# Sample scores woven into the prompt's attention, and output products between the sample's values

## The reference, cut to what matters

```
z = rmsnorm(x) @ w_in            # u | q | k | v, 4 heads, q and k in two halves of 64
s = q @ k / 8 - slope * dist     # per head and half; masked where dist < 0
p = softmax(s)
o = (p[half 0] - lam * p[half 1]) @ v
o = rmsnorm(o) * g * 0.8
x = x + [pool_out ; o] @ w_out
x = x + moe_top4of32(rmsnorm(x)) # router, 32 experts, clamped SwiGLU
y = rmsnorm(x)
```

## Time and profile before

| | us |
|---|---|
| median of 3 runs | 1681.72 |
| lowest, highest | 1679.38, 1684.91 |
| the profiled execution's own time | 1682.89 |
| its span | 1681.1 |
| TensorE busy | 1542.0 (92%) |
| VectorE busy | 1223.2 (73%) |
| ScalarE busy | 1004.1 (60%) |

### The profile page before, as it was taken

One profiled execution on the slowest core, in us unless ns is written; L12 is line 12 of the kernel. 1 busy time (PEld: TensorE's weight loads), 2 busy tenths in 40 slices (PEclk: granted clock), 3 DMA queues, 4 the chain that ended last, 5 costly groups with the idle time before them and its releaser, 6 DMA issues.

```text
span 1681.1 us, 23490 instructions
## 1 busy us (share of the span) xinstructions
PE 1542.0 (92%) x7948; PEld 1275.0 (76%) x7949; DVE 1223.2 (73%) x1035; ACT 1004.1 (60%) x894; POOL 435.1 (26%) x404
## 2 busy tenths in 40 slices
PE   5799669997599999999999999999999999999960
PEld 5799344887478888888888888888888888888850
DVE  3312860226478888888888888888888888888848
ACT  4322554014367677767767776776776677677632
POOL 1000000000422332333233233223323322332311
PEclk9899679998799999999999999999999999999985
DMA  7233115431588999999999999999999999998936
GB/s 219 84 101 115 64 51 160 160 129 60 233 307 340 360 355 345 360 359 364 361 361 356 346 360 357 366 359 363 358 346 363 358 365 357 361 360 343 354 108 257
DMA packets 93472, 475.98 MB, mean 283 GB/s; under 512 B 14410, under 2 KB 27354, under 8 KB 43665
## 3 DMA queue, kind: packets, MB, share of 16 engines
q1 hardware_dynamic: 81689, 449.85, 71.4%
q0 software_dynamic: 11744, 25.61, 4.0%
HBM read 468.62 MB, written 23.74 MB: 293 GB/s over the span
## 4 chain that ended last, share of the span: by engine, by line
PE 84%; DVE 8%; DMA 3%; ACT 2%; issue 1%; POOL 1%; SPq 0%; POOLq 0%; DVEq 0%; ACTq 0%
PE ps L1614 62%; PE ps L1350 8%; PE ps L1593 3%; PE ps L1619 3%; PE ps L1511 2%; DVE arena L1314 2%; PE ps L1487 2%; DVE lo L940 1%; DMA raw<-w_in 1%; PE ps L1472 1%; PE ps L1587 1%; ACT hi L642 1%; DMA arena<-h_rows,idx_g 1%; DVE arena L1037 1%; DVE stats L1041 1%
## 5 line engine op out<-in xcount | busy, mean ns | idle before, releaser
L940 DVE TENSOR_TENSOR lo<-raw,hi 128x2048 fp32r<-128x2048 f32 x268 | 605.7, 2289 | 129.9 <-ACT hi L642 129.8
L642 ACT ACTIVATE hi<-raw 128x2048 fp32r<-128x2048 f32 x268 | 499.0, 1909 | 107.3 <-PE ps L1614 65.1
L1614 PE MATMUL ps<-hi,t_hi 128*128 128x512 f32 x1536 | 447.6, 400 | 6.9 <-DVE t_lo L1217 5.2
L1614 PE MATMUL ps<-lo,t_hi 128*128 128x512 f32 x1536 | 434.8, 391 | 0.0
L1614 PE MATMUL ps<-hi,t_lo 128*128 128x512 f32 x1536 | 434.4, 391 | 0.0
L1614 PEld LDWEIGHTS ps<-lo,t_hi 128*128 128x128 f32 x1536 | 289.7, 189 | 62.9
L1614 PEld LDWEIGHTS ps<-hi,t_lo 128*128 128x128 f32 x1536 | 289.9, 189 | 61.4
L1614 PEld LDWEIGHTS ps<-hi,t_hi 128*128 128x128 f32 x1536 | 280.4, 189 | 70.5 <-DVE lo L940 11.4
L940 DVE TENSOR_TENSOR lo<-arena,hi 128x2048 fp32r<-128x2048 f32 x128 | 290.3, 2288 | 20.8 <-ACT hi L642 20.7
L642 ACT ACTIVATE hi<-arena 128x2048 fp32r<-128x2048 f32 x128 | 245.4, 1917 | 47.1 <-PE ps L1614 46.1
L577 POOL COPY idx_g<-idx 128x1 uint32 (+1 forms) x34 | 71.7, 2110 | 361.2 <-PE ps L1593 328.3
(11 more groups left out here) (223 smaller groups left out, 1391.0 us busy)
## 6 DMA issues: line engine op xcount, KB each, us to landing
raw<-w SPq DMA_DIRECT2D x256, 1024.0 KB, 5.7
arena<-w SPq DMA_DIRECT2D x128, 1024.0 KB, 7.5
raw<-w_in SPq DMA_DIRECT2D x8, 1024.0 KB, 5.5
raw<-cache_k SPq DMA_DIRECT2D x32, 256.0 KB, 3.5
raw<-cache_v SPq DMA_DIRECT2D x32, 256.0 KB, 3.3
raw<-w_out SPq DMA_DIRECT2D x4, 1024.0 KB, 4.9
arena<-expert_rows SPq DMA_DIRECT2D x2, 2048.0 KB, 14.1
hi<-expert_rows SPq DMA_DIRECT2D x2, 2048.0 KB, 22.9
```

Of the source, the lines that this page charges most:

```text
L642: act_e.activation(hi[:, slot, :], raw_at(slot_raw), ACT.Copy).then_inc(s_hi, 1)
L940: v.tensor_tensor(lo[:, slot, :], raw_at(slot_raw), hi[:, slot, :].bitcast(F32), ALU.subtract).then_inc(s_lo, 1)
L1614: last = pe.matmul(ps[:, base_bank + b, :], lhs[l][:, row, :], r[:, ck.slot(j), at:at + 512], start=first_k and kk == 0 and q == 0, stop=F ...
```

## The change

The sample's 32 page steps no longer follow the attention: two are placed ahead of its loop and two in each step. For this the PSUM banks are dealt anew: the scores have two banks (one step) instead of four, the transposed weights one instead of two, the values bank 3, the transposed page one instead of three. ScalarE's copies of the pages (`page_t`) stand one ahead and one behind `weights_t` in each step. The products with the new keys are a block of their own behind the loop (`new_key_scores`). For a finished column block, `o_squares`, `o_norm` and `o_lo` move from steps 1, 2 and 4 behind it to steps 0, 1 and 3. The table of the sample's weights (`p_t`) is laid out with a wider step. Behind the loop both sample softmaxes precede `o_norm(3)`, `out_product(0)` starts the next stage, sequences 4 to 7 of the values are placed between the router's work, and the last `choose` steps are in another order. POOL's reloads of x wait for the new-key scores in addition.

```diff
+        B_AT, B_PV, B_KT = 2, 3, 4
+
+        def o_bank(i):
+            return 5 if i < 4 else 7
...
             pool.wait_ge(s_qb, 2)
             pool.wait_ge(s_sss, NB * H)
+            pool.wait_ge(s_nk, 1)
             reload_x(2, s_xr[1])
...
+            def page_t(m):
+                act_e.wait_ge(s_kp, m + 1)
+                if m >= 2:
+                    act_e.wait_ge(s_sss, m - 1)
+                act_e.activation(kt_s[:, m % 2, :], ps[:, B_KT, :], ACT.Copy).then_inc(s_kc, 1)
+
+            page_t(0)
+            page_t(1)
+            for i in range(16):
+                exponents(i)
+                if i < 15:
+                    page_t(2 * i + 2)
+                weights_t(i)
+                if i < 15:
+                    page_t(2 * i + 3)
+                if i >= 5 and i % 4 == 1:
+                    o_root(i // 4 - 1, P)
+                if i >= 7 and i % 4 == 3:
+                    o_hi(i // 4 - 1)
...
+            sample_exp(0)
             sample_exp(1)
+            o_root(3, P)
+            o_hi(3)
...
             bias_max(0)
+            sample_queries()
             for i in range(16):
                 if i + 1 < 16:
                     bias_max(i + 1)
                 weights(i)
-                if i == 2:
-                    sample_queries()
+                if i % 4 == 0 and i >= 4:
+                    v.wait_ge(s_pv, i)
+                    o_squares(i // 4 - 1)
                 if i % 4 == 1 and i >= 5:
-                    v.wait_ge(s_pv, i - 1)
-                    o_squares(i // 4 - 1)
-                if i % 4 == 2 and i >= 6:
                     o_norm(i // 4 - 1)
-                if i % 4 == 0 and i >= 8:
-                    o_lo(i // 4 - 2)
-            o_lo(2)
+                if i % 4 == 3 and i >= 7:
+                    o_lo(i // 4 - 1)
...
             sample_softmax(0)
             sample_softmax(1)
+            o_norm(3)
+            residual(0)
+            o_lo(3)
             sample_weights(0)
-            residual(0)
-            v.wait_ge(s_kp, NB * H + 4 * H)
-            o_squares(4)
-            o_norm(4)
-            sample_weights(1)
-            residual(1)
             start = Chunks(PRO, 0)
             v.wait_ge(s_late2, 64)
             v.memset(before[:, 0, :], 0.0)
             link(v.memset(sel, 0.0))
             norm2(0)
-            o_lo(4)
+            residual(1)
+            sample_weights(1)
+            norm2(1)
+            v.wait_ge(s_kp, NB * H + 4 * H)
+            o_squares(4)
             residual(2)
-            norm2(1)
+            o_norm(4)
+            norm2(2)
+            choose(0)
+            choose(1)
             v.wait_ge(s_kp, 2 * NB * H)
             o_squares(5)
             o_norm(5)
+            o_lo(4)
             residual(3)
             o_lo(5)
-            norm2(2)
-            choose(0)
-            residual(4, (0, 1))
             norm2(3)
-            choose(1)
-            residual(4, (2, 3))
+            choose(2)
+            residual(4)
             norm2(4)
-            choose(2)
             choose(3)
             choose(4)
...
-                if i >= 2:
-                    pe.wait_ge(s_sb, i - 1)
+                if i >= 1:
+                    pe.wait_ge(s_sb, i)
...
-                if m >= 3:
-                    pe.wait_ge(s_kc, m - 2)
+                if m >= 1:
+                    pe.wait_ge(s_kc, m)
...
+            def new_key_scores():
+                pe.wait_ge(s_ate, 16)
+                for m in range(NB * H):
+                    b, h = m // H, m % H
+                    rows = slice(32 * (b % 4), 32 * (b % 4) + 32)
+                    last = pe.matmul(ps[rows, B_AT, 32 * (b // 4):32 * (b // 4) + 32], q_blk[:, m, :], k_t[:, h, 512:544], start=h == 0, stop=h == H - 1,
+                                     tile_position=(0, 32 * (b % 4)))
+                last.then_inc(s_nk, 1)
+
+            pe.wait_ge(s_pl, 4)
+            scores(0)
+            page_transposes(0)
+            scores(1)
+            sample_scores(0)
+            sample_scores(1)
...
+            for i in range(16):
+                if i + 2 < 16:
+                    scores(i + 2)
+                if i >= 1:
+                    values(i - 1)
+                if i < 15:
+                    sample_scores(2 * i + 2)
+                weight_transposes(i)
+                if i < 15:
+                    sample_scores(2 * i + 3)
+            values(15)
+            new_key_scores()
...
+            out_product(0)
+            o_transposes(3, P)
+            sample_transposes(0)
+            out_product(1)
+            sample_transposes(1)
+            for b in range(4):
+                sample_values(b)
             out_product(2)
             pe.wait_ge(s_late2, 64)
             h2_transposes(0)
-            out_product(3)
+            sample_values(4)
             router(0)
+            sample_values(5)
+            h2_transposes(1)
+            sample_values(6)
+            router(1)
+            sample_values(7)
+            o_transposes(4, P)
+            out_product(3, (0, 1))
+            h2_transposes(2)
+            out_product(3, (2, 3))
             o_transposes(5, P)
-            h2_transposes(1)
+            router(2)
             out_product(4, (0, 1))
-            router(1)
-            h2_transposes(2)
-            out_product(4, (2, 3))
-            router(2)
             h2_transposes(3)
+            out_product(4, (2,))
+            router(3)
+            out_product(4, (3,))
             h2_transposes(4)
-            router(3)
             router(4)
```

More of the change, by code:

```diff
@@ L734, in o_hi, with exponents @@
                     act_e.activation(sample_cols(t_hi, i - 4), every_32(src), ACT.Copy).then_inc(s_oh_, 1)
+            def exponents(i):
+                nk = P * (i // 4 + 1)
+                act_e.wait_ge(s_mx, i + 1)
+                for c in range(2):
+                    w = pr[:, 2 * (i % 2) + c, 0:nk]
+                    e = act_e.activation(w, w, ACT.Exp, bias=st[:, 20 + 2 * (i % 2) + c:21 + 2 * (i % 2) + c],
+                                         accum_out=st[:, 24 + 2 * (i % 2) + c:25 + 2 * (i % 2) + c])
+                e.then_inc(s_e, 1)
             def weights_t(i):
@@ L741, in weights_t @@
                     act_e.wait_ge(s_pv, i - 1)
[L742 to L759, removed]
+                act_e.activation(at_sb[:, i % 2, 0:nk], ps[:, B_AT, 0:nk], ACT.Copy).then_inc(s_ate, 1)
+            def page_t(m):
[16 more added lines that the diff above has]
+                    o_hi(i // 4 - 1)
             act_e.wait_ge(s_ust, 32)
@@ L1425, in scores, with weight_transposes @@
                 nk = P * (qt + 1)
-                if i >= 2:
-                    pe.wait_ge(s_sb, i - 1)
+                if i >= 1:
+                    pe.wait_ge(s_sb, i)
                 for c in range(2):
                     rows = slice(HD * c, HD * c + HD)
-                    last = pe.matmul(ps[:, 2 * (i % 2) + c, 0:nk], q_t[rows, h, P * qt:P * qt + P], k_t[rows, h, 0:nk], start=True, stop=True)
+                    last = pe.matmul(ps[:, c, 0:nk], q_t[rows, h, P * qt:P * qt + P], k_t[rows, h, 0:nk], start=True, stop=True)
                 last.then_inc(s_sc, 1)
+            def weight_transposes(i):
+                pe.wait_ge(s_a, i + 1)
+                if i >= 1:
+                    pe.wait_ge(s_ate, i)
+                for k in range(i // 4 + 1):
+                    last = pe.transpose(ps[:, B_AT, P * k:P * k + P], aa[:, i % 2, P * k:P * k + P], ident)
+                last.then_inc(s_atr, 1)
             def o_transposes(i, n):
@@ L1476, in _, with sample_scores @@
[L1476 to L1479 removed]
+            def sample_scores(m):
                 b, h = m // H, m % H
[L1481 to L1482 removed]
                 if m + 1 < NB * H:
                     page_transposes(m + 1)
+                if m == 0:
+                    pe.wait_ge(s_qb, 2)
                 pe.wait_ge(s_kc, m + 1)
                 rows = slice(32 * (b % 4), 32 * (b % 4) + 32)
[L1487 to L1489 removed]
+                pe.matmul(ps[rows, 6 + b // 4, :], q_blk[:, m, :], kt_s[:, m % 2, :], start=h == 0, stop=h == H - 1,
@@ L1548, in router @@
                 last.then_inc(s_lg, 1)
-            for t in range(2):
-                sample_transposes(t)
-                out_product(t, (0, 1))
-                sample_values(4 * t)
-                out_product(t, (2, 3))
-                for b in range(4 * t + 1, 4 * t + 4):
-                    sample_values(b)
-            o_transposes(4, P)
+            out_product(0)
[5 more added lines that the diff above has]
+                sample_values(b)
             out_product(2)
```

108 lines of the change are left out of this document (41 added, 67 removed).

## The result

| | kernel before | changed kernel |
|---|---|---|
| median | 1681.01 us (4 runs, 1679.38 to 1684.91) | 1700.58 us (4 runs, 1699.02 to 1701.97) |
| span of the profiled execution | 1681.1 us | 1697.2 us |
| mean granted clock | 0.955 | 0.961 |

The ratio is 1.012, 95% interval 1.010 to 1.014: **slower by some 20 us**, where 2.2 us less were forecast, and outside the range of 1670 to 1691. The forecast is wrong, and the sign with it.

What follows compares the result with a forecast made beforehand. VectorE was taken to bound the attention, TensorE the page stage and the woven loop. 12.0 us gained in the loop, less 3.8 behind it and 6 for clock falls, left 2.2 us gained: 1679.5 us, range 1670 to 1691.

Steps and rivals of the forecast that it cites:

- loop with its block: Woven attention loop through the new-key scores: 109.0 us at full clock where it was 121.0, 12.0 us gained.
- part two: From behind the new-key scores to the router's running sums: 3.8 us lost at full clock.
- the clock falls (two and one): TensorE clock drops at long stalls: three of five possible places, 2 us lost each, 6 us together.
- After that each wait that I followed had been met: Behind the wait in out_product(0), TensorE's followed waits, norm2 among them, were already met: no further loss.
- Content without the new-key scores: TensorE's own work in the woven loop at full clock, apart from the new-key products: 74.5 us.
- The new-key block: 32 new-key products in a block behind the loop, 0.155 us each: 5.0 us.
- The wait in every step: Second page transposition waits for ScalarE's page copy behind weights_t: 0.9 to 1.25 us in 15 steps, 15.8 us.
- The norm of o: TensorE stalls at steps 5, 9 and 13 while VectorE's o_norm awaits ScalarE's root: 8.5 us together.
- `o_lo` and the ends: Score waits at steps 7 and 11, the last step's weights, and the start: 5.2 us together.
- The wait in `out_product(0)`: Third chunk waits for the first residual, behind both softmaxes and o_norm(3) on VectorE: 3.9 us.
- The tail: From the last output product to the router's running sums: 9.1 us, 5.0 less than before.
- the rival by which it does not come back: TensorE's clock stays at 0.50 early in the woven loop, with later falls: slower, 1692 us; chance 0.20.

Runs made afterwards that it cites:

- store ahead of the wait: Changed kernel with GpSimd's stores of h2 of tiles 0 and 1 issued ahead of the wait for the sample's last value; 1679.61 us, 0.9984 of before.
- store in its place, loads behind it: Changed kernel with SyncE's first expert-weight loads also waiting until the first store of h2 has landed; 1691.05 us, 1.0049 of before.
- part one alone: Changed kernel's woven loop and new-key block, then the earlier kernel's order except two output-product chunks and o_transposes(3) moved ahead; 1679.64 us, 0.9981 of before.
- pages first: "store ahead of the wait" with both page copies of a step ahead of the transposed weights' copy on ScalarE; 1671.32 us, 0.9940 of before.
- norm later: "pages first" with o_norm one step later on VectorE and o's transpositions one step later on TensorE; 1665.25 us, 0.9907 of before.
- residual first: "norm later" with residual(0) split and its first chunks placed earlier in VectorE's queue, behind each softmax; 1660.89 us, 0.9864 of before.
- page before the exponentials: "residual first" with the first page copy ahead of the exponentials on ScalarE at steps 6, 10 and 14; 1659.09 us, 0.9856 of before.

## Why the prediction was wrong, step by step

Measured over the same three points (loop with its block; part two; both), in us. The end of the block is its row's end or the start of the next product, 0.07 us apart, so a tenth is open in the first two columns:

| | loop | part two | both |
|---|---|---|---|
| kernel before | 121.0 | 122.7 | 243.7 |
| forecast, with the clock falls (two and one) | 113.0 | 128.5 | 241.5 |
| changed kernel | 112.3 | 148.2 | 260.5 |
| store ahead of the wait | 114.1 | 128.2 | 242.3 |
| store in its place, loads behind it | 114.0 | 140.8 | 254.9 |
| part one alone | 112.3 | 129.7 | 242.0 |
| pages first | 101.8 | 128.2 | 230.0 |
| norm later | 98.3 | 129.8 | 228.2 |
| residual first | 99.9 | 123.3 | 223.2 |
| page before the exponentials | 97.2 | 123.4 | 220.6 |

- **The step that failed** is the sentence "After that each wait that I followed had been met". The wait of `norm2(2)` for the store of tile 0 was not followed into GpSimd's queue, past the wait for the last value. The sum put it at nothing, and it cost some 19 us of the 148.2; with the store ahead part two is 128.2 for a forecast of 128.5. The forecast had looked at this queue once, for the reloads at its front, and not at what stands at its end. The size has a second part: the loads of the experts' weights, let go by the same value, stretched the store's landing from 3.2 to 10.5 us. This one term gave the forecast its wrong sign.
- **The loop** came out as summed, 112.3 for 113.0, but in part by luck, since its terms were off in both directions. Content without the new-key scores: 84.6 us busy for 74.5, the largest error in the loop. About 3 us of it are the clock, which the forecast had as a term of its own; the page products take 0.98 us from start to start in the woven order (244.49 to 245.47) where 0.88 was read in the earlier trace rows, 3 us over 32; the rest, about 4 us, was not followed row by row. The waits together were 26 us for a forecast of 29.5. The new-key block took 1.4 us instead of 5.0: its price was read from products that stand alone between larger ones, and 64 in a row go through in 1.51 us, 24 ns each. The Trainium skill, page TensorE: Matmul & The Clock Gate, section Back-to-back issue gap, puts products of up to 64 columns at about 25 ns; the trace agrees, and by an estimate from that figure, 64 times 25 ns, the term would have been 1.6 us.
- **The wait in every step**: forecast 15.8 us, measured 14.5 in 14 waits of 0.86 to 1.27, all released by the page copy, and all gone with ScalarE's order.
- **The norm of o**: forecast 2.65, 2.9 and 2.0 + 0.95 us, measured 2.37, 2.64, 1.71 and 0.81. The root without a drain was the right choice. **`o_lo` and the ends**: forecast 5.2; measured 0.58 and 0.85 us at the scores, 1.18 and 0.69 in the last step and 0.63 at the start, 3.9 together.
- **The wait in `out_product(0)`**: forecast 3.9 us, measured 4.67 and, with the store ahead, 3.87. **The tail**: from the last product's end to the sums 9.1 us forecast, 9.0 measured.
- **The clock**: three falls of 2 us were forecast, out of five places. Three came in the loop and in `out_product(0)`, in the windows from 212 to 220, 276 to 284 and 292 to 300 us, 1.7 us each by an estimate from what the windows lack to 1.00: at the first stall of the norm, at the third with the two shorter waits after it, and at the wait of 4.67 us. The second stall of the norm, the longest with 2.64 us at 241.74, brought no fall. A fourth fall, from about 384 to 404, came with the gap of 6.42 us that the sum did not have. In the kernel before the clock stood at 0.50 for the first 26 us of the loop; here it was at 1.00 from 176 to 212, so the rival by which it does not come back fell. Its sign was right and its mechanism was not. The forecast's reading of the kernel before also left out a stretch at 0.50, from 214 to 219 us, behind a gap of 2.74 us that ends at 211.92.
- **The scale.** Where the queue is mended, 1.4 us are gained by the trace and 0.5 to 4.9 by the medians' interval, against 2.2 forecast.

The windows of the changed kernel that the bullet on the clock rests on (columns as above):

```profile
212.00:216.00 4.00, 3.86 (x17) 2.69 (x18) 3.79 (x9) 0.58 (x3) 0.00 (x0) 0.66 0.00 0
216.00:220.00 4.00, 2.95 (x10) 0.76 (x8) 0.55 (x4) 2.33 (x7) 0.00 (x0) 0.92 0.78 255
...
240.00:244.00 4.00, 2.26 (x15) 1.50 (x16) 3.83 (x9) 2.11 (x6) 0.00 (x0) 1.00 0.00 0
...
276.00:280.00 4.00, 2.82 (x11) 1.42 (x9) 0.93 (x4) 2.48 (x6) 0.00 (x0) 0.76 0.61 196
280.00:284.00 4.00, 3.31 (x40) 2.79 (x40) 1.68 (x3) 1.09 (x2) 0.32 (x1) 0.81 0.02 4
...
292.00:296.00 4.00, 0.36 (x2) 0.40 (x3) 2.97 (x8) 1.48 (x2) 0.00 (x0) 0.90 0.45 172
296.00:300.00 4.00, 4.00 (x26) 4.00 (x26) 0.00 (x0) 0.00 (x0) 0.00 (x0) 0.68 0.02 4
```

## What to carry to other kernels

When an edit moves an instruction ahead in one queue, take every wait that it has, find the instruction elsewhere that releases it, and read that engine's queue backwards from there to the last wait: a transfer issued behind a wait on unrelated work is only as early as that work, and here it cost some 19 us, where the whole change was forecast to gain 2. Then look at what else the same event lets go, since those transfers share the way. And when TensorE has become the bound of a loop, look at the order of the copies on the engine that empties PSUM: here that order alone took 12.3 us from the loop, and with two more edits of order (the norm, the residual) the two parts lost 19 us, against 1.4 us by the trace and some 3 by the medians for the change itself with its store ahead. Whether the same edits help without the weaving was not tried.

## What the runs showed of the hardware that was not expected

- A store of 512 KB issued by GpSimd landed in 3.2 us beside a reload of 128 KB, and in 10.5 us behind three loads of 1 MB that SyncE issued 0.8 us before it (308 GB/s in that window).
- Products of 128 rows by 32 columns, 64 in a row, took 24 ns each; two of them standing between larger products took 0.15 us of TensorE's time.
- A wait of 2.37 us on TensorE was followed by a clock of 0.66 in the next 4 us, one of 2.64 by 1.00 throughout (changed kernel, 212 and 242 us). In the run with the store ahead, whose loop has the same code and the same two waits, it was the other way round: 1.00 behind the 2.37 us at 209.84, and 0.67 in the window from 240 to 244 behind the 2.64 us at 237.82. The length of the idle gap alone does not tell whether the clock falls: one and the same loop had its fall at one gap in one execution and at another in the next.
